# Reordering two groups of small matmuls in a gated-linear-attention mixer: heads on the outside instead of array tiles in turn

## The reference

```
q_dec = q * exp(b);  k_intra = k * exp(-b);  k_state = k * exp(b_last - b)
attn = where(mask, q_dec @ k_intra.T, 0)          # inside a chunk
o_intra = attn @ v
chunk_kv = k_state.T @ v                          # (64 x 128) per head and chunk
s_next = decay * s + chunk_kv                     # scan over the chunks, both directions
o = o_intra + q_dec @ s_start
```

## Time and profile before

| | |
|---|---|
| median of 3 runs | 1741.15 us (1739.62 to 1742.61) |
| the profiled execution | 1739.62 us, with a span of 1737.5 us |
| PE busy | 1672.4 us, 96% of the span |
| DVE, ACT, POOL busy | 375.6, 185.3, 135.3 us |
| mean granted clock of PE | 0.982 |
| transfers | 628.22 MB |

### The profile page before, as it was taken

One profiled execution on the slowest core, in us unless ns is written; L12 is line 12 of the kernel. 1 busy time (PEld: TensorE's weight loads), 2 busy tenths in 40 slices (PEclk: granted clock), 3 DMA queues, 4 the chain that ended last, 5 costly groups with the idle time before them and its releaser, 6 DMA issues.

```text
span 1737.5 us, 43008 instructions
## 1 busy us (share of the span) xinstructions
PE 1672.4 (96%) x19754; PEld 1036.3 (60%) x19754; DVE 375.6 (22%) x695; ACT 185.3 (11%) x295; POOL 135.3 (8%) x204
## 2 busy tenths in 40 slices
PE   6998879799999999999999999999999999999997
PEld 3787558433434356666666666666668787444443
DVE  5431573611111102020202020202020111111113
ACT  4331451200000000000000000000000000000001
POOL 1000020120101010101000000000000001010000
PEclk9999989799999999999999999999999999999999
DMA  8620842999999999999999999999999999999995
GB/s 314 218 79 1 301 150 108 366 389 416 407 417 408 416 408 417 408 416 408 416 408 415 410 410 414 400 416 399 412 403 412 396 416 398 419 399 418 395 418 243
DMA packets 123341, 628.22 MB, mean 362 GB/s; under 512 B 11197, under 2 KB 14098, under 8 KB 106794
## 3 DMA queue, kind: packets, MB, share of 16 engines
q1 hardware_dynamic: 111872, 598.74, 85.3%
q0 software_dynamic: 10256, 23.91, 4.7%
q10 hardware_dynamic: 1050, 2.97, 0.4%
HBM read 609.37 MB, written 16.21 MB: 360 GB/s over the span
## 4 chain that ended last, share of the span: by engine, by line
PE 87%; DMA 6%; DVE 3%; ACT 1%; issue 1%; SPq 1%; ACTq 0%; DVEq 0%; POOLq 0%
PE bank L1782 48%; PE bank L1794 17%; PE bank L1796 8%; DMA ring<-in_w_e_up 3%; PE bank L1369 3%; PE bank L1370 3%; PE bank L1371 3%; DMA ring<-in_w_e_gate 1%; PE bank L1396 1%; SPq L444 1%; PE bank L1681 1%; DMA raw<-in_w_out 0%; PE bank L1391 0%; DMA pos_col<-in_pos 0%; DVE S L1093 0%
## 5 line engine op out<-in xcount | busy, mean ns | idle before, releaser
L1782 PE MATMUL bank<-ring,xe 128*32 128x352 f32 x12288 | 917.6, 460 | 5.2 <-DVE xe L1293 3.1
L1782 PEld LDWEIGHTS bank<-ring,xe 128*32 128x32 f32 x12288 | 557.7, 110 | 359.4 <-issue 160.9
L1794 PE MATMUL bank<-ring,hidT 128*32 128x512 f32 x2816 | 385.5, 592 | 0.0
L1796 PE MATMUL bank<-ring,hidT 128*32 128x256 f32 x2816 | 235.4, 379 | 0.0
L1796 PEld LDWEIGHTS bank<-ring,hidT 128*32 128x32 f32 x2816 | 129.5, 110 | 172.6 <-issue 172.6
L1300 DVE TENSOR_TENSOR hid<-sg,bank 128x1056 f32<-128x1056 f32 x32 | 40.1, 1255 | 829.9 <-PE bank L1782 829.9
L1794 PEld LDWEIGHTS bank<-ring,hidT 128*32 128x32 f32 x2816 | 127.4, 110 | 29.3 <-issue 2.5
L881 ACT ACT_TABLE_LOAD x16 | 20.5, 1283 | 867.4 <-PE bank L1782 867.4
L643 POOL DMA_INDIRECT acc_dram<-yab,idx_s x15 | 24.3, 1622 | 1028.9 <-DVE yc L1311 1028.9
L1309 DVE SCALAR_TENSOR_TENSOR yab<-bank,gate_cur,gfab 128x512 f32<-128x512 f32 x16 | 12.0, 751 | 330.4 <-PE bank L1796 330.4
L881 ACT ACTIVATE sg<-bank 128x1056 f32<-128x1056 f32 x32 | 33.6, 1051 | 420.6 <-PE bank L1782 420.5
(11 more groups left out here) (262 smaller groups left out, 772.3 us busy)
## 6 DMA issues: line engine op xcount, KB each, us to landing
ring<-in_w_e_gate SPq DMA_DIRECT2D x128, 1408.0 KB, 25.2
ring<-in_w_e_up SPq DMA_DIRECT2D x128, 1408.0 KB, 25.0
ring<-in_w_e_down SPq DMA_DIRECT2D x96, 1536.0 KB
ring<-in_w_e_down SPq DMA_DIRECT2D x32, 1024.0 KB
raw<-in_w_ada SPq DMA_DIRECT2D x16, 1024.0 KB, 6.2
raw<-in_w_in SPq DMA_DIRECT2D x8, 1024.0 KB, 5.5
ada_f<-in_w_ada SPq DMA_DIRECT2D x4, 1024.0 KB, 16.5
raw<-in_w_out SPq DMA_DIRECT2D x4, 1024.0 KB, 8.4
```

Source lines behind the costliest of these rows:

```text
L1782: last = nc.tensor.matmul(bank[b][32 * g:32 * g + 32, 0:GCOLS], xe[:, t, c, :], w[:, n, GCOLS * g:GCOLS * g + GCOLS], start=c == 0, stop=c ...
L1794: nc.tensor.matmul(bank[6][r:r + 32, :], hidT[:, ph, t, c, :], w[:, n, 512 * h:512 * h + 512], start=first, stop=stop)
L1796: last = nc.tensor.matmul(bank[7][32 * g:32 * g + 32, 0:256], hidT[:, ph, 2, c, :], w[:, n, 256 * g:256 * g + 256], start=first, stop=stop)
```

## The change

Two loops of the matrix engine's program are reordered. The matmuls, their operands and their results are the same, except that in `o_rows` the four state matmuls of a head are added in another order.

In `gla_3` chunk `ch` is now outermost: first all eight matmuls of chunk 0 (directions, then heads, so that `par` alternates), then all eight of chunk 1. Each half signals `g_kv` when it is done; before, both counts came near the end.

In `o_rows` the heads are outermost: for each head one whole-array matmul, then chunk 0 with both directions, then chunk 1 with both directions.

```
-                for q in range(4):
-                    for ch in range(2):
-                        rows_ = slice(ch * CHUNK, (ch + 1) * CHUNK)
-                        for par in range(2):
-                            h = 2 * (q % 2) + par
-                            last = nc.tensor.matmul(bank[7 - ch][par * DK:par * DK + DK, q * DV:(q + 1) * DV],
-                                                    kst[rows_, s, q, par * DK:par * DK + DK],
+                for ch in range(2):
+                    rows_ = slice(ch * CHUNK, (ch + 1) * CHUNK)
+                    for a in range(2):
+                        for h in range(HEADS):
+                            hp, par = divmod(h, 2)
+                            last = nc.tensor.matmul(bank[7 - ch][par * DK:par * DK + DK, (2 * a + hp) * DV:(2 * a + hp + 1) * DV],
+                                                    kst[rows_, s, 2 * a + hp, par * DK:par * DK + DK],
                                                     proj[rows_, t, 1, h * DV:(h + 1) * DV], start=True, stop=True)
-                        if q == 3:
-                            last.then_inc(g_kv, 1)
+                    last.then_inc(g_kv, 1)
...
             def o_rows(t):
-                for hp in range(HP):
-                    for par in range(2):
-                        h = 2 * hp + par
-                        nc.tensor.matmul(o_bank(t, par)[:, hp, :], attn[:, t, h, :], proj[:, t, 1, h * DV:(h + 1) * DV], start=True, stop=False)
-                    for a in range(2):
-                        for ch in range(2):
-                            tok = slice(ch * CHUNK, (ch + 1) * CHUNK)
-                            for par in range(2):
-                                r = slice(par * DK, par * DK + DK)
-                                last = nc.tensor.matmul(o_bank(t, par)[tok, hp, :], qdec[r, t, 2 * a + hp, tok],
-                                                        S[r, state_slot(t, ch, a, True), hp, :], start=False, stop=a == 1)
+                for h in range(HEADS):
+                    hp, r = h // 2, slice(h % 2 * DK, h % 2 * DK + DK)
+                    cols = slice(h * DV, (h + 1) * DV)
+                    out = o_bank(t, h % 2)[:, hp, :]
+                    nc.tensor.matmul(out, attn[:, t, h, :], proj[:, t, 1, cols], start=True, stop=False)
+                    for ch in range(2):
+                        tok = slice(ch * CHUNK, (ch + 1) * CHUNK)
+                        for a in range(2):
+                            last = nc.tensor.matmul(out[tok, :], qdec[r, t, 2 * a + hp, tok],
+                                                    S[r, state_slot(t, ch, a, True), hp, :], start=False, stop=a == 1)
                 last.then_inc(o_ps, 1)
```

## The result

| | before | after |
|---|---|---|
| median | 1741.77 us (4 runs, 1739.62 to 1742.61) | 1757.61 us (4 runs, 1755.98 to 1759.83) |
| ratio of the runs | | 1.0090, 95% interval 1.0078 to 1.0102 |
| profiled execution, span | 1739.62 us, 1737.5 us | 1758.52 us, 1756.4 us |
| mean granted clock | 0.982 | 0.975 |

The change costs 15.8 us; forecast were 7.3 and a range that ended at 1753.0. The direction was right, the size was not. The 19 executions of the changed kernel on record take 1754.41 to 1761.66 us at a mean clock of 0.973 to 0.978, so the profiled one stands for all of them.

A forecast was written before the change was run, and what follows sets the result against it. PE was taken to bound the kernel, busy 96% of the span, with both loops partly on the path. 2.6 us (gla_3) + 4.7 (o_rows) = 7.3 on 1741.15 gave 1748.5 us, range 1743.8 to 1753.0.

The forecast's parts named there:

- the first 4 us of o_rows: Start of o_rows at granted clock 0.57: one token tile done as before, so increments stay those at full clock.
- The recorded sign of being wrong: In o_rows: the forecast is wrong if a head takes over 1.3 us; 1.13 was expected.
- The clock rival: Half-clock stretches of the chain, together worth 8.6 us, may find the clock up; net -4 to +4 us, chance 0.10.
- Part 2, the order itself: o_rows: 1.13 us a head, +2.04 a token tile; term +4.7 us, ends 3.2 and 6.5.
- The strict-order rival: o_rows: second quarter starts with the first's last pass; total +11.3 us, 1752.5; chance 0.15 together with no overlap.
- the deep look-ahead for gla_3: Rival: engine looks past 16 waiting passes, gla_3 stays at 0.86 us; total +3.2 us, 1744.4; chance 0.15.
- Whole-array stage: o_rows, per head: two whole-array passes take 0.64 - 2 x 0.11 = 0.42 us.
- Part 1, gla_3: gla_3: two quarters at work instead of four, +0.86 us a turn; term +2.6 us, ends 0 and 3.0.
- the fourth in the wait: gla_3's fourth turn: its added 0.86 us falls into PE's 0.85 us wait for attn ahead of gla_2(4).
- What is on the path: o_rows: scalar engine waits for two token tiles, +4.1 us; waiting 0.6 for tile 3 makes it 4.7.
- Mixed(0, 0, 1): After o_rows on PE: 12 matmuls at full clock, 0.23 us each, 2.7 us, ending just in time at 251.5.
- Pass-through to the end: After o_rows: every delay at 247 us reaches the end undiminished, as PE and transfers of the expert stage shift along.

The follow-up runs named there:

- e2: Only the o_rows reorder, gla_3 as in the kernel before: 1757.54 us, ratio 1.0092 to the kernel before.
- e3: The changed kernel with five unused 128x512 float32 matmuls in PE's idle time ahead of o_rows: 1741.47 us, ratio 1.0008 to the kernel before.
- e4: The kernel before with five unused 128x512 float32 matmuls ahead of o_rows: 1740.43 us, ratio 1.0000.
- e10: The kernel before with gla_3 giving each quarter of the array its eight passes in one run: 1745.01 us, one run.
- e5: gla_3 as before; o_rows head by head, each head's state matmuls alternating between its two quarters: 1757.62 us, ratio 1.0095 to the kernel before.
- e6: The kernel before with o_rows still in head pairs, but its quarter matmuls one quarter after the other, four passes each: 1740.01 us, ratio 0.9994.
- e1: Only the gla_3 reorder, o_rows as in the kernel before: 1741.5 us, ratio 1.0007 to the kernel before.
- e12: The changed kernel with 20 unused matmuls spread over PE's idle times on the path: 1739.38 us, ratio 1.0002 to the kernel before.
- e8: The kernel before with 20 unused matmuls spread over PE's idle times on the path: 1736.12 us, ratio 0.9973.
- e7: The kernel before with each head pair's quarter stage in o_rows cut in two by an unused whole-array matmul: 1752.85 us, ratio 1.0068.
- e9: The kernel before with the odd heads' quarter matmuls in o_rows left out, so two of four quarters work: 1743.33 us, ratio 1.0029.
- e11: The changed kernel with five unused 128x512 float32 matmuls between the first and second token tile of o_rows: 1749.94 us, ratio 1.0064 to the kernel before.

## Why the prediction was wrong

**The step that failed** is the sentence on the first 4 us of o_rows: "I let them do the same amount of work now, so the increments stay those at full clock." It takes the time of the clock's rise from the kernel before and treats it as given, though the work that brought the rise is the very work that was changed. Measured: no rise in 35.6 us (e2, the changed kernel), at full clock the same matmuls take 20.2 (e3). The recorded sign of being wrong, a head of over 1.3 us, came up: 1.78. Of the 21.7 us by which o_rows grew, 15.4 are the clock and 6.3 the order itself (7.8 against the 12.4 of e4, where the old order starts at full clock too).

**The clock rival** stood in the forecast, but only on the side where it gives time back. I looked at stretches that were at half clock and might gain, and not at one that had risen before and might no longer.

**Part 2, the order itself.** Quarter stage of a head: 0.71 taken, with ends of 0.60 and 0.82; 0.59 measured (e3), the lower end. The look-ahead is three waiting passes a quarter (e10), just what a head needs. The strict-order rival (0.93 for the quarter stage) is refuted by that 0.59 and by e5 and e6, the deep look-ahead for gla_3 by 1.52 us a turn. Whole-array stage 0.42: as forecast. With it the term would have been 3.2.

**Part 1, gla_3.** +0.86 a turn taken, +0.49 measured (1.52 against 1.03), since the second chunk's quarters begin while the first's last three rounds run. Three turns on the path and the fourth in the wait was right as far as gla_2(4): it starts 36.37 us after the first L1541 in e1 and 34.84 in the kernel before, 1.5 more, which is 3 x 0.49. PE still waited 0.37 us for attn ahead of it. How much of the 1.5 reaches the end is not shown: the start of o_rows scatters by more than that, and e1's time gives 1.2, with an interval from -0.5 to 3.0.

**What is on the path.** The forecast said that only two token tiles count, that the cover of the others is thin, and that beyond 2.04 us a token tile each further us costs about five. That is what happened: at +4.6 a token tile PE's end sets the time, the wait for tiles 2 and 3 is 5.87 us long, and the chain runs through o_rows to its end. Mixed(0, 0, 1) was put at full clock, 2.7 us; it ran at half, 5.0.

**Pass-through to the end**: +20.4 at L1702, +18.9 at the end. The router stage gave 2.1 back, since it found the clock up earlier, and 0.6 came up elsewhere. Right but for that. The sum with the measured sizes and a clock that is no worse than before is 3.2 + 1.5 = 4.7; e12 against e8 gives 4.3.

The page "TensorE: Matmul & The Clock Gate" of the Trainium skill, Part 1, says that half rate is the default, and that how busy the engine has been lately releases it. As far as that the traces agree. By its advice to avoid idle gaps o_rows should have risen, since the profile shows PE busy for all of the 35.5 us in the three stretches above; it did not.

## What to carry to other kernels

Where a stretch begins at half clock, ask whether the work in it can raise the clock before taking any of its durations over from another order; price it at both levels. With small float32 matmuls that share the array, this case speaks for keeping all parts of it busy and for grouping them so that the array is seldom re-partitioned (e7, e9). A wait ahead of such a stretch can be filled with unused whole-array matmuls: here that was worth some 15 us for the changed kernel (e3) and, over all waits on the path, 0.27% for the kernel before.

## What the runs showed of the hardware that was not expected

- The clock has a memory: the same 200 records ran at 0.50 for 35.3 us after a cold start (e2) and at 1.00 for 20.2 us after a warm one (e3), and in e11 both states follow each other in one execution.
- The old order rose from half clock 3.7 us (before), 6.5 (e1) and 6.3 (e6) after its start; the new order did not in 35.
- Either doubled changes of mode (e7) or an idle half of the array (e9) keeps it from rising, with PE shown as busy the whole time. In e6, with neither, it rose. What exactly the chip counts is left open.
- Passes on different quarters start out of program order, with up to three passes waiting on a quarter (e10 and the changed kernel); four in a row on each cost 0.62 us against 0.60 in turn (e6).
